# Token-tile turns with a diagonal of roots, and expert slots in the order in which they come free, in a two-block transformer kernel

## The chip, the cores and the metric

The kernel runs on one core of one Trainium2 chip. The metric is the device time of one execution in microseconds, from three runs; one further execution was profiled. The engines are TensorE (PE in the rows), VectorE (DVE), ScalarE (ACT), GpSimd (POOL) and SyncE (SP), which here issues all transfers.

## The reference, cut to what matters

256 tokens of width 1024 pass through two layers of a first block and one hybrid layer of a second, all in float32:

```python
for i in range(2):                      # mixer 0: MLA attention, mixer 1: differential attention
    a = mixer_i(rms_norm(h, norm_g[i, 0]))
    h = h + rms_norm(a, norm_g[i, 1])
    f = conv_ffn(rms_norm(h, norm_g[i, 2]))      # 1024 -> 2 x 2816, conv of 3 tokens, gelu gate, -> 1024
    h = h + rms_norm(f, norm_g[i, 3])
# second block
a = rms_norm(h, g_mix)                  # then a projection by w_in, two attentions, gates, w_out
h = h + mixed @ w_out
h = h + hier_moe(rms_norm(h, g_ffn))    # 32 experts of 1024 -> 512 -> 1024, each token takes 2
out = rms_norm(h, g_final)
```

`rms_norm(x, g)` is `x * rsqrt(mean(x * x) + eps) * g`. The router sends each of the 256 tokens to two experts; the kernel streams all 32 experts' w1, w3 and w2 (2 MB each, 96 matrices).

## The kernel before

**Products.** A weight piece of up to 128x2048 is loaded into `raw` (4 buffers), ScalarE writes its high part and POOL its low part (`high`, `low`, 4 buffers), and TensorE makes each product of three matmuls: high x high, high x low, low x high (`product`, L669 to L671). The activations lie likewise as `xh` and `xl`, transposed, features on the partitions. `low_ready` counts finished pieces, `pieces_used` the pieces that TensorE has read; it is raised by the first product after a piece.

**Stages and turns.** The order of work is written out by hand, once per engine, and `plan()` gives each group of products a bank of PSUM. Between the stages lie turns, named by what they prepare: `x1` (MLA attention to first FFN), `x2` (FFN to differential attention), `x3` (attention to second FFN), `x4` (FFN to the hybrid layer). A turn has these steps. ScalarE squares the four banks of the branch (`out_sums`, L1316), VectorE multiplies each by the gain `gpost` (`post`, L1784), adds the sums and refines the reciprocal root that ScalarE guessed (`refined`, L1709 to L1717), and adds the branch to the residual `h`, one instruction for each tile of 128 tokens (L1796). ScalarE squares `h` (`h_sums`), the root is refined again, and VectorE writes `xn = h * root * gpre` in four halves (`normed`, L1760). TensorE transposes 16 blocks (`x_transposed`, L679), ScalarE copies the high parts (L1347) and VectorE subtracts for the low parts (L1736); then the products of the next stage begin. In `x4` the root isn't in the path: `xn = h * gpre` (`x_gained`), and the root is applied later. Meanwhile TensorE runs 32 dummy products (`keep_clock`, L698). All steps but the first squares are made for both tiles together:

```python
refined(st[:, 16:18], st[:, 18:20])
for t in range(NT):
    dve.scalar_tensor_tensor(h[:, t, :], xn[:, t, :], st[:, 16 + t:17 + t], h[:, t, :],
                             ALU.mult, ALU.add).then_inc(h_ready, 1)
```

The last products of the attention stages finish tile 0's two banks first; the last `down` piece of an FFN goes over the hidden tiles outermost. The gain rows `gpre` and `gpost` are loaded by SyncE (`pre_gains`, `post_gains`), each behind a wait for the last use.

**Expert slots.** The expert matrices go into eight slots of 2 MB, in turn. They overlay the piece buffers: slot 0 is a part of `room`, 1 and 2 are pairs of `raw` buffers, 3 to 6 the four `parts` buffers, 7 is `xspare`. Matrix n goes into slot n modulo 8. `vacated(c)` is SyncE's wait before the first use of a slot; later uses wait for `slots_used`, which TensorE raises when it has read a w1, w3 or w2 pair. SyncE is one queue: a wait holds everything behind it. Experts are taken in pairs (six matrices); TensorE's products are at L1237 and L1262, the gather of tokens at L1187.

## Time and profile before

| what | value |
|---|---|
| median of three runs | 1347.19 us (1344.73 to 1347.28) |
| the profiled execution: time, span | 1345.34 us, 1343.5 us |
| mean granted TensorE clock | 0.994 |
| busy: PE, DVE, ACT, POOL | 95%, 38%, 41%, 43% of the span |
| chain that ended last: PE, transfers, ACT, DVE | 75%, 13%, 4%, 4% |
| POOL's low part of a piece, mean | 4466 ns, 128 of them |
| ScalarE's high part of a piece, mean | 1853 ns, 128 of them |
| HBM read | 339.10 MB |

Shares are averages over very different stages. The chain that ended last says what held the end at each time, and the windows say how busy an engine was in each stage; both are needed here.

### The profile page before, as it was taken

Reading aid. Unit: us, or ns where it says so; the run is one execution under the profiler, and the core shown is the slowest. Engines: PE = TensorE matmul, PEld = TensorE weight load, DVE = VectorE, ACT = ScalarE, POOL = GpSimd, SP = SyncE. Lnnn points to the kernel's source line nnn. Section 1 sums busy time; section 2 is a strip of 40 time slices with the busy share of each in tenths; the row PEclk is TensorE's granted clock in tenths of the full one; section 3 lists DMA queues with packets and bytes.
Section 4 is the critical chain, followed back from the end, with each engine's and each line's share of the span. In section 5 each row is a group of like instructions: output and inputs, shape, how many; then the busy total and the mean of one; then the engine's idle time right before and its main releaser. Section 6 shows DMA issues by size and latency. Waiting matters only on the chain.

```text
span 1343.5 us, 20032 instructions
## 1 busy us (share of the span) xinstructions
PE 1282.8 (95%) x7959; PEld 954.6 (71%) x7959; DVE 509.6 (38%) x1303; ACT 548.0 (41%) x853; POOL 573.2 (43%) x136
## 2 busy tenths in 40 slices
PE   6999999999998899999999999999999999999996
PEld 6867999998987799999878888854444444454442
DVE  2434444445265454444657453421111111121112
ACT  4654555556477465555543664311111111111112
POOL 4722788885944188888567855200000000000001
PEclk9999999999999999999999999999999999999998
DMA  8731666664633266664446444599999999999994
GB/s 270 235 94 63 182 195 188 190 199 144 220 126 95 63 203 196 196 188 165 149 165 203 159 137 161 230 421 426 427 428 428 429 428 429 429 429 428 429 423 189
DMA packets 156933, 341.22 MB, mean 254 GB/s; under 512 B 8537, under 2 KB 119482, under 8 KB 144314
## 3 DMA queue, kind: packets, MB, share of 16 engines
q1 hardware_dynamic: 156858, 340.18, 68.1%
q8 instruction: 53, 0.87, 0.3%
q14 instruction: 22, 0.18, 0.0%
HBM read 339.10 MB, written 1.05 MB: 253 GB/s over the span
## 4 chain that ended last, share of the span: by engine, by line
PE 75%; DMA 13%; ACT 4%; DVE 4%; POOL 2%; issue 1%; SPq 0%; ACTq 0%; DVEq 0%
PE bank L669 16%; PE bank L671 15%; PE bank L670 15%; PE bank L1237 11%; DMA xspare<-in_w 6%; DMA ring<-in_w 6%; PE bank L1262 5%; PE bank L1187 3%; PE bank L768 2%; POOL parts L621 2%; PE bank L679 1%; PE bank L1217 1%; ACT parts L1305 1%; PE bank L1105 1%; PE bank L1121 1%
## 5 line engine op out<-in xcount | busy, mean ns | idle before, releaser
L621 POOL TENSOR_TENSOR parts<-raw,parts 128x2048 fp32r<-128x2048 f32 (+4 forms) x128 | 568.0, 4466 | 290.2 <-ACT parts L1305 290.2
L669 PE MATMUL bank<-xh,parts 128*128 128x256 f32 x1032 | 288.0, 279 | 6.0 <-POOL parts L621 4.0
L670 PE MATMUL bank<-xl,parts 128*128 128x256 f32 x1032 | 285.9, 277 | 0.0
L671 PE MATMUL bank<-xh,parts 128*128 128x256 f32 x1032 | 285.8, 277 | 0.0
L1305 ACT ACTIVATE parts<-raw 128x2048 fp32r<-128x2048 f32 (+4 forms) x128 | 236.1, 1853 | 23.4 <-PE bank L669 8.5
L1237 PE MATMUL bank<-ring,room 128*64 128x512 f32 x768 | 226.1, 594 | 7.1 <-DMA ring<-in_w 4.5
L644 POOL TENSOR_TENSOR xn<-h,gpost 128x512 f32<-128x512 f32 x4 | 4.9, 1270 | 474.7 <-DVE h L2258 474.7
L669 PEld LDWEIGHTS bank<-xh,parts 128*128 128x128 f32 x1032 | 194.2, 188 | 12.6 <-POOL parts L621 4.8
L670 PEld LDWEIGHTS bank<-xl,parts 128*128 128x128 f32 x1032 | 193.8, 188 | 0.8
L671 PEld LDWEIGHTS bank<-xh,parts 128*128 128x128 f32 x1032 | 193.9, 188 | 0.0
L1237 PEld LDWEIGHTS bank<-ring,room 128*64 128x64 f32 x768 | 72.5, 137 | 111.4 <-issue 111.4
L669 PE MATMUL bank<-parts,xh 128*128 128x512 f32 (+5 forms) x304 | 114.7, 377 | 5.8 <-DVE xl L1738 2.2
L1262 PE MATMUL bank<-ring,room 128*64 128x512 f32 x384 | 115.0, 600 | 0.7 <-ACT room L1668 0.7
L671 PE MATMUL bank<-parts,xl 128*128 128x512 f32 (+5 forms) x304 | 112.5, 370 | 0.0
L670 PE MATMUL bank<-parts,xh 128*128 128x512 f32 (+5 forms) x304 | 112.2, 369 | 0.0
L1668 ACT ACTIVATE room<-bank 128x512 f32<-128x512 f32 x16 | 9.6, 597 | 193.5 <-PE bank L1248 193.5
L671 PE MATMUL bank<-parts,hl 128*128 128x512 f32 x192 | 75.6, 394 | 0.0
L669 PE MATMUL bank<-parts,hh 128*128 128x512 f32 x192 | 74.6, 389 | 0.8 <-POOL parts L621 0.8
L670 PE MATMUL bank<-parts,hh 128*128 128x512 f32 x192 | 75.3, 392 | 0.0
L1484 ACT ACTIVATE room<-bank,room 128x256 f32<-128x256 f32 x64 | 32.7, 560 | 102.2 <-PE bank L671 101.0
L1342 ACT ACTIVATE room<-bank 128x512 f32<-128x512 f32 (+1 forms) x75 | 41.1, 581 | 75.9 <-PE bank L679 32.5
L1262 PEld LDWEIGHTS bank<-ring,room 128*64 128x64 f32 x384 | 34.9, 138 | 51.5 <-issue 49.3
(255 smaller groups left out, 1858.9 us busy)
## 6 DMA issues: line engine op xcount, KB each, us to landing
ring<-in_w SPq DMA_DIRECT2D x67, 2048.0 KB, 22.9
raw<-in_ffn_w_up SPq DMA_DIRECT2D x88, 512.0 KB, 4.9
room<-in_w SPq DMA_DIRECT2D x12, 2048.0 KB, 20.3
raw<-in_ffn_w_down SPq DMA_DIRECT2D x44, 512.0 KB, 3.9
xspare<-in_w SPq DMA_DIRECT2D x11, 2048.0 KB, 26.6
raw<-in_w_in SPq DMA_DIRECT2D x40, 512.0 KB, 4.1
raw<-in_diff_w_qkv SPq DMA_DIRECT2D x24, 512.0 KB, 4.6
ring<-in_w SPq DMA_DIRECT2D x10, 1024.0 KB, 24.8
```

Source lines behind the costliest of these rows:

```text
L621: pool.tensor_tensor(low[:, p % PARTS, 0:n], raw[:, p % RING, 0:n], high[:, p % PARTS, 0:n], ALU.subtract).then_inc(low_ready, 1)
L669: first = pe.matmul(out_, a[0], b[0], start=start, stop=False)
L670: pe.matmul(out_, a[0], b[1], start=False, stop=False)
L671: return first, pe.matmul(out_, a[1], b[0], start=False, stop=stop)
L679: ins = pe.transpose(b[0:cols, at:at + rows], src, ident[0:rows, 0:rows])
L768: ins = pe.matmul(b[:, t * S:t * S + S], qs[n][:, t * P:t * P + P], ks[n], start=n == 0, stop=n == len(qs) - 1)
L1187: ins = pe.matmul(bank[2 + k // 4][:, P * (k % 4):P * (k % 4) + P], xn[:, t, P * k:P * k + P], Sel[:, t].rearrange("p e c -> p (e c)"), st ...
L1237: ins = pe.matmul(bank[x][CAP * e:CAP * e + CAP, :], XgT[:, k, CAP * e:CAP * e + CAP], rows_of(j, x, e, k, EF), start=k == 0, stop=k == KT ...
L1262: ins = pe.matmul(bank[1 + hf][CAP * e:CAP * e + CAP, :], hidT[:, k, CAP * e:CAP * e + CAP], rows_of(j, 2, e, k, D)[:, 512 * hf:512 * hf + ...
L1305: act.activation(high[:, p % PARTS, 0:n], raw[:, p % RING, 0:n], ACT.Copy).then_inc(high_ready, 1)
L1342: act.activation(dst, src, func, scale=scale).then_inc(bank_moved[BANK[g]], 1)
L1484: act.activation(fbuf[b][a], bank[b][:, a * S:a * S + S], ACT.Identity, bias=par(3, a), scale=par(1, a)).then_inc(centre, 1)
```

## The change

**Turns.** `post` becomes `turned_over`: gained halves, sums, root and residual of tile 0, then those of tile 1; the last `down` piece of an FFN finishes tile 0 first. In x1 to x3 `xn` and its gain are gone: VectorE writes a diagonal of the tile's roots (`spread_roots`), and TensorE multiplies each 128x128 block of `h` by it (`h_transposed`), which transposes and scales. The gain of the features is now a column (`gcol`, loaded as 32 rows with the parameters and transposed once) and is applied in the high and low parts, which go by chunks of 128x256 (`high_chunks`, `low_chunks`); the next stage waits for one bank at a time. x4 transposes `h` unscaled. The dummy products are 23 in x1 to x3, and 5 and 11 in x4. Four of the six loads of `gpre` are gone, and with them SyncE's waits.

**Slots.** The slots are renumbered in the order in which they come free (third and fourth slot are now `parts` buffers), and the ninth matrix of the first four pairs goes into two free places of 1 MB (`ninth`), once the router has read `xT`, ahead of the wait for its slot. Its slot stays empty for that turn. `cs` now also holds `prow` and `convT`, so that the second place is in one piece.

```diff
-        slots += [pairs_of[tail[2 * x] // 2] for x in range(RING // 2)]
-        slots += [pairs_of[RING // 2 + b] for b in tail]
+        slots += [pairs_of[tail[0] // 2]]
+        slots += [pairs_of[RING // 2 + b] for b in tail[:2]]
+        slots += [pairs_of[tail[2] // 2]]
+        slots += [pairs_of[RING // 2 + b] for b in tail[2:]]
         slots += [xspare[:, :]]
+        NINTH = (1, 1, 0)
+        ninth = [view(4096, HALF), cs[:, C_DIST:C_DIST + HALF]]
...
             def vacated(c):
+                end = W["end"]
                 if c == 0:
                     full(sp, A_["hyb_att"][2][7])
-                elif c < 3:
-                    sp.wait_ge(low_ready, W["end"] - RING + 2 * c)
+                elif c in (1, 4):
+                    sp.wait_ge(low_ready, end - 2 if c == 1 else end)
                 else:
-                    sp.wait_ge(pieces_used, W["end"] - RING + min(c - 3, RING - 1) + 1)
+                    sp.wait_ge(pieces_used, {2: end - 3, 3: end - 2, 5: end - 1}.get(c, end))
...
+                            elif begins and (j, x, e) == NINTH:
+                                full(sp, G["router1"])
+                                for n in range(2):
+                                    sp.dma_start(ninth[n].unsqueeze(1), w[:, 2 * j + e:2 * j + e + 1, HALF * n:HALF * n + HALF]
+                                                 ).then_inc(ninth_here, 16)
+                                continue
+                            elif e == 0 or begins and (j, x) == NINTH[:2]:
                                 sp.wait_ge(slots_used, 12 * four + (3 * j + x - SLOTS // 2 + 1))
...
+            def h_transposed(name, site, scaled, between=0):
+                b = [begin(G[name] + q) for q in range(4)]
+                for t in range(NT):
+                    if t and between:
+                        keep_clock(between, bank[4])
+                    if scaled:
+                        pe.wait_ge(spread_ready, 2 * (site - 1) + t + 1)
+                    else:
+                        pe.wait_ge(h_ready, 2 * (site - 1) + t + 1)
+                    for k in range(KT):
+                        at = S * (k % 2) + P * t
+                        dst, src = b[k // 2][:, at:at + P], h[:, t, P * k:P * k + P]
+                        if scaled:
+                            ins = pe.matmul(dst, src, spread_r[:, t], start=True, stop=True)
+                        else:
+                            ins = pe.transpose(dst, src, ident)
+                        if t == 0 and k == 0:
+                            behind(ins)
+                        if t and k % 2:
+                            end(ins, G[name] + k // 2)
+                late.extend([(2 * q, G[name] + q) for q in range(4)])
...
-            WAIT = 32
+            WAIT = 23
...
-                if k == 4:
-                    while late:
-                        moved(pe, late.pop(0))
+                while late and late[0][0] <= k:
+                    moved(pe, late.pop(0)[1])
...
+                    each = [(x, t, hf) for x in range(2) for t in range(NT) for hf in range(2)]
+                    if stop:
+                        each = [(x, t, hf) for t in range(NT) for x in range(2) for hf in range(2)]
+                    for i, (x, t, hf) in enumerate(each):
+                        if not any(x == y for y, _, _ in each[:i]):
+                            pe.wait_ge(hid_ready, n + (n0 + 1 + x))
+                        first, ins = product(bank[4 + 2 * t + hf][:, :],
+                                             [y[:, (j + x) % 4, t * P:t * P + P] for y in (hh, hl)],
+                                             [y[:, x, 512 * hf:512 * hf + 512] for y in w],
+                                             start and x == 0, stop and x == 1)
+                        behind(first)
+                        if stop and x == 1:
+                            ins.then_inc(ffn_full, 1)
...
-            keep_clock(WAIT, bank[3])
-            x_transposed("x4", 4)
+            keep_clock(WAIT // 4, bank[3])
+            h_transposed("x4", 4, False, WAIT // 2)
...
+                            if nine and (j, x, e) == NINTH and k == KT - 1:
+                                ins.then_inc(arrived[slot_of(*NINTH)[0]], 16)
...
+                    if by_tile:
+                        act.wait_ge(h_squares, 2 * site + t + 1)
+                        guess(st[:, 28 + t:29 + t], st[:, t:t + 1], D)
+                if not by_tile:
+                    act.wait_ge(h_squares, 2 * site + 2)
+                    guess(st[:, dst:dst + 2], st[:, 0:2], D)
...
+            def high_chunks(name, site):
+                for k in range(KT):
+                    g = G[name] + k // 2
+                    full(act, g)
+                    act.activation(xh[:, k, :], bank[BANK[g]][:, S * (k % 2):S * (k % 2) + S], ACT.Copy,
+                                   scale=gain_of(site, k)).then_inc(x_high, 1)
...
+                    squares(st[:, 2 + n:3 + n], bank[b][:, :], view(6400 + 512 * n, 512), post_squares)
+                    if n % 2:
+                        t = n // 2
                         outs_done[0] += 1
-                    squares(st[:, 2 + n:3 + n], bank[b][:, :], view(6400 + 512 * n, 512), post_squares)
-                act.wait_ge(sums_ready, outs_done[0])
-                guess(st[:, 16:18], st[:, 18:20], D)
+                        act.wait_ge(sums_ready, outs_done[0])
+                        guess(st[:, 16 + t:17 + t], st[:, 18 + t:19 + t], D)
...
+            def low_chunks(name, site):
+                for k in range(KT):
+                    g = G[name] + k // 2
+                    x_parts[0] += 1
+                    dve.wait_ge(x_high, x_parts[0] + (1 - k % 2))
+                    ins = dve.scalar_tensor_tensor(xl[:, k, :], bank[BANK[g]][:, S * (k % 2):S * (k % 2) + S],
+                                                   gain_of(site, k), xh[:, k, :], ALU.mult, ALU.subtract)
+                    if k % 2:
+                        ins.then_inc(bank_moved[BANK[g]], 1)
...
+            def half_of(t, src):
+                steps[0] += 1
+                dve.tensor_scalar(st[:, 32 + t:33 + t], src, -0.5 / D, -0.5 * EPS, ALU.mult, ALU.add).then_inc(vec, 1)
+            def root_of(t, y):
+                guesses[0] += 1
+                dve.wait_ge(guessed, guesses[0])
+                dve.wait_ge(vec, steps[0])
+                a = st[:, 48 + t:49 + t]
+                link(dve.tensor_scalar(a, y, y, st[:, 32 + t:33 + t], ALU.mult, ALU.mult))
+                link(dve.tensor_scalar(y, a, 1.5, y, ALU.add, ALU.mult))
+            def turned_over(site, banks, ring_groups):
+                def gained_half(t, hf):
+                    b = banks[2 * t + hf]
+                    dve.wait_ge(post_squares, 4 * site + 2 * t + hf + 1)
+                    x = slice(512 * hf, 512 * hf + 512)
+                    ins = dve.tensor_tensor(xn[:, t, x], bank[b][:, :], gpost[:, x], ALU.mult)
                     ins.then_inc(bank_moved[b] if ring_groups else vec, 1)
-                if not ring_groups:
-                    steps[0] += 4
-                sums = st[:, 2:6].rearrange("p (t h) -> p t h", h=2)
-                dve.tensor_tensor(st[:, 18:20], sums[:, :, 0], sums[:, :, 1], ALU.add).then_inc(sums_ready, 1)
-                dve.wait_ge(sums_ready, site + 1)
-                refined(st[:, 16:18], st[:, 18:20])
-                for g in ring_groups or []:
-                    moved(dve, g)
-                for t in range(NT):
+                    if not ring_groups:
+                        steps[0] += 1
+                def summed(t):
+                    dve.wait_ge(post_squares, 4 * site + 2 * t + 2)
+                    dve.tensor_tensor(st[:, 18 + t:19 + t], st[:, 2 + 2 * t:3 + 2 * t], st[:, 3 + 2 * t:4 + 2 * t],
+                                      ALU.add).then_inc(sums_ready, 1)
+                    dve.wait_ge(sums_ready, 2 * site + t + 1)
+                    half_of(t, st[:, 18 + t:19 + t])
+                def residual(t):
+                    root_of(t, st[:, 16 + t:17 + t])
+                    for g in (ring_groups or [])[2 * t:2 * t + 2]:
+                        moved(dve, g)
                     dve.scalar_tensor_tensor(h[:, t, :], xn[:, t, :], st[:, 16 + t:17 + t], h[:, t, :],
                                              ALU.mult, ALU.add).then_inc(h_ready, 1)
+                dve.wait_ge(gpost_here, 16 * (site + 1))
+                gained_half(0, 0)
+                summed(0)
+                gained_half(0, 1)
+                residual(0)
+                gained_half(1, 0)
+                summed(1)
+                gained_half(1, 1)
+                residual(1)
+            def spread_roots(site):
+                for t in range(NT):
+                    dve.wait_ge(h_squares, 2 * site + t + 1)
+                    half_of(t, st[:, t:t + 1])
+                    root_of(t, st[:, 28 + t:29 + t])
+                    dve.tensor_scalar(spread_r[:, t], ident, st[:, 28 + t:29 + t], None, ALU.mult).then_inc(spread_ready, 1)
+            def x_transposed(name, site):
+                spread_roots(site)
+                low_chunks(name, site)
```

## Rows read from the trace of the kernel before

**Rows 1.** Windows by stage: length, busy us (instructions) by engine, clock, DMA share, GB/s.

```profile
132.50:315.50 183.00, 181.08 (x1320) 170.08 (x1321) 85.19 (x204) 102.92 (x130) 151.26 (x33) 1.00 0.62 189
657.40:865.30 207.90, 205.03 (x1328) 177.03 (x1329) 108.71 (x270) 105.47 (x164) 132.10 (x29) 1.00 0.48 163
890.00:1100.00 210.00, 209.92 (x1148) 99.05 (x1146) 39.12 (x83) 26.90 (x37) 0.00 (x0) 1.00 1.00 427
1100.00:1320.00 220.00, 211.15 (x1134) 101.47 (x1130) 37.04 (x81) 28.18 (x38) 0.00 (x0) 1.00 1.01 426
```

**Rows 2.** TensorE's waits from 130 to 315 us: total, times, longest.

```profile
PE bank L669 <- POOL parts L621: 1.9, 1, 1.9
```

**Rows 3.** Timeline of turn x1: start, us, engine, line, operation [idle before].

```profile
118.44 0.19 ACT L1316 ACTIVATION_READ_ACCUMULATOR room<-bank 128x1 f32 x1
...
120.50 7.46 PE L698 MATMUL bank<-xh 128*128 128x512 f32 x32
...
123.47 2.48 DVE L1796 SCALAR_TENSOR_TENSOR h<-xn,st,h 128x1024 f32<-128x1024 f32 x2
...
126.96 0.18 ACT L1316 ACTIVATION_READ_ACCUMULATOR xn<-h 128x1 f32 x1
...
127.58 0.46 DVE L1714 TENSOR_SCALAR st<-st 128x1 f32<-128x1 f32 x2 [0.19 <-ACT st L1330]
...
128.44 2.74 DVE L1760 SCALAR_TENSOR_TENSOR xn<-h,st,gpre 128x512 f32<-128x512 f32 x4
...
132.47 0.35 PE L669 MATMUL bank<-xh,parts 128*128 128x256 f32 x1 [0.59 <-issue]
```

**Rows 4.** Timeline of turn x4.

```profile
646.36 2.68 DVE L1784 TENSOR_TENSOR xn<-bank,gpost 128x512 f32<-128x512 f32 x4 [3.37 <-ACT room L1316]
...
647.43 7.45 PE L698 MATMUL bank<-xh 128*128 128x512 f32 x32
...
654.71 1.91 PE L679 MATMUL bank<-cs,xn 128*128 128x128 f32 x16
...
657.37 0.36 PE L669 MATMUL bank<-parts,xh 128*128 128x256 f32 x1 [0.75 <-DVE xl L1736]
```

**Rows 5.** Timeline at the end of the first FFN, ahead of turn x2.

```profile
310.67 0.42 DVE L1973 TENSOR_TENSOR hl<-bank,hh 128x256 fp32r<-128x256 f32 x1
...
311.41 0.39 PE L669 MATMUL bank<-parts,hh 128*128 128x512 f32 x1
```

**Rows 6.** ScalarE copies out of PSUM, by form: ns min/median/max.

```profile
L1342 ACT ACTIVATE room<-bank x75: 378/597/624, 36.1 to 870.2; 128x512 f32<-128x512 f32 x70, 128x256 f32<-128x256 f32 x5
L1342 ACT ACTIVATE room<-bank,st x4: 677/686/688, 709.8 to 757.0; 128x512 f32<-128x512 f32 x4
```

**Rows 7.** TensorE's timeline at the first gather of the experts.

```profile
877.67 3.81 PE L1187 MATMUL bank<-room,xn 128*128 128x128 f32 x32 [1.52 <-DVE room L2223]
```

**Rows 8.** Timeline of the first tile after turn x1.

```profile
138.40 1.02 ACT L1484 ACTIVATE room<-bank,convT 128x256 f32<-128x256 f32 x2 [5.88 <-PE bank L671]
...
139.46 0.87 DVE L1957 SCALAR_TENSOR_TENSOR room<-bank,convT,room 128x255 f32<-128x255 f32 x2 [5.89 <-ACT room L1484]
```

**Rows 9.** SyncE's issues of expert matrices, from narrow timelines.

```profile
888.59 0.33 SPq L578 DMA_DIRECT2D room<-in_w  x1
...
896.57 0.80 SPq L578 DMA_DIRECT2D ring<-in_w  x2
...
908.22 0.80 SPq L578 DMA_DIRECT2D ring<-in_w  x2
```

**Rows 10.** Narrow windows, columns as in rows 1.

```profile
890.00:891.00 1.00, 1.00 (x8) 0.37 (x6) 0.37 (x2) 0.00 (x0) 0.00 (x0) 1.00 0.61 197
910.00:911.00 1.00, 1.00 (x6) 0.29 (x4) 0.00 (x0) 0.00 (x0) 0.00 (x0) 1.00 0.94 344
446.00:449.00 3.00, 3.00 (x8) 2.35 (x8) 0.15 (x1) 0.69 (x2) 2.65 (x1) 0.50 0.00 0
```

**Rows 11.** TensorE's timeline ahead of the slow stretch at 446.

```profile
445.44 0.50 PE L669 MATMUL bank<-parts,xh 128*128 128x512 f32 x1 [1.56 <-DVE xl L1738]
```

131 lines of the change are left out of this document (56 added, 75 removed).

## The prediction

> **What bounds the kernel now.** I read the granted clock first (0.994 over the span), then the chain of work that ended last, then busy time by windows. The windows show two regimes [rows 1]. From the first FFN to the router TensorE is busy 181.1 of 183.0 us and 205.0 of 207.9 us, and the waits that remain are small and hang on its own earlier progress: the one of the first FFN, 1.9 us, is for the third piece's low part [rows 2], which ScalarE begins only after the first tile's products, so it moves with them. In the expert stage the transfers run at 427 GB/s from 890 us to the end while TensorE is busy 209.9 of 210.0 us and later 211.2 of 220 us: from about 1100 us each pair waits a little for data, so the end is set by the expert stream. One matrix is 2.097 MB, so 4.9 us at that rate. The stream is held by TensorE at its start: a slot is refilled when products free it.
>
> Between stages lie four turns, in which TensorE runs only 32 dummy products, transposes and nothing else. In turn x1 the dummies start at 120.50 and the first product of the next stage at 132.47: 11.97 us [rows 3]. x2 and x3 have the same 11.97 in their timelines. x4 takes 657.37 - 647.43 = 9.94 us, as its gain and transposes don't wait for a root [rows 4]. The reader should see that everything between is a single chain over DVE and ScalarE: residual, squares, root, gain, transpose, high part, low part, each for both tiles before the next begins.
>
> **The turn, part by part.** Times are from the first dummy.
> 1. *The roots of the branch by tile.* The second square of tile 0 is read at 118.63, -1.87 [rows 3]. DVE then has, in order: add and half 0.35, gained half 0.67 (four in 2.68 [rows 4]), root 0.55, residual 1.24 (two in 2.48 [rows 3]), and for tile 1 gained half 0.67, add and half 0.35, gained half 0.67, root 0.55, residual 1.28. The sum is 6.33, so both residuals end at +4.46 instead of +5.45 (123.47 + 2.48). The root for both tiles took 128.44 - 127.58 = 0.86 [rows 3]; with one tile two dependent operations remain, bounds 0.43 and 0.86, and 0.55 is nearer the lower, because it is two latencies without the second issue. Squares of tile 0 lie beside all this. Queued behind ScalarE's new waits is only this chain.
>    For x2 and x4 the last down piece is reordered, tile 0 first. That gives them tile 0's banks as early as x1 and x3 have them. It asks for the second hidden tile two products earlier: low part done at 311.09, third product at 311.41 [rows 5], so 0.3 us to spare, the same in both FFNs.
> 2. *The diagonal of roots.* After the residual ScalarE squares tile 1: it ended 1.19 us after the residual (126.96 + 0.18 against 125.95) [rows 3]. Then guess to DVE 0.44 (127.14 to 127.58), root 0.55, and a 128x128 diagonal, for which I take 0.3, between half of a pair of one-column operations (0.23 [rows 3]) and one of 255 columns (0.475 [rows 8]). Diagonal ready: 4.46 + 1.19 + 0.44 + 0.55 + 0.3 = +6.94. The four 512-wide gains (2.74 in all) leave the path.
> 3. *Scaled transposes.* These are full products of 128 columns; 32 such in the gather took 3.81 [rows 7], 0.119 each, the same as transposes [rows 4]. Tile 0's eight lie in the wait. After tile 1's first two (0.24 + 0.15 to the end) a bank is full: +7.35.
> 4. *Chunks of 128x256 with a gain column.* ScalarE's plain copy of that size is 0.378 and a scale from a column adds 0.09 at 512 (0.686 against 0.597) [rows 6], so 0.47, a pitch of 0.37 (two with scale and bias 0.46 apart, 0.56 long [rows 8]). DVE's like operation is 0.475 long at a pitch of 0.40 [rows 8]. A bank has two chunks and DVE waits for both highs: 0.37 + 0.47 + 0.40 + 0.475 + hand-overs 0.15 = 1.87. TensorE starts at +9.22 instead of +11.97, 2.75 sooner.
> 5. *Then it takes the banks as they come.* Six products last 0.70, a bank's two lows 0.80: three times 0.10 is lost. Net 2.45 per turn. Slow end: chunks as L1484 (0.56, pitch 0.46) and pairs at 0.95, diagonal 0.5: 1.6. Fast end: chunk times without the column's surcharge, no loss: 2.9. I take 2.4; three turns 7.2 (4.8 to 8.7).
> 6. *x4.* Tile 1 is transposed at the later of +4.46 and +4.63 (16 dummies of 0.23 and 8 transposes of 0.119), first bank +5.05, plus 1.87: +6.92 against 9.94, minus 0.1: 2.9 (2.3 to 3.2). Squares and scales follow the chunks on ScalarE and come perhaps 1.5 us sooner, not 3; the third piece of w_in still has some 1.5 us of cover, and if the cover is gone up to 1 us of the 2.9 is lost.
>
> *What is removed and moved on queues.* Four 512 KB gain loads go, four loads of 8 rows come, a gain copy and 32 more transposed rows ride with the parameters in the attention stage. SyncE no longer waits for the normed halves behind the gain loads, so the weights of the next stage are issued up to 6 us sooner; TensorE isn't waiting for them, so this counts nothing, 0 to 0.3 us either way.
>
> **The slots.** The new order lets the third and fourth slot fill while wout's products run, where the transfers stood idle; the ninth matrix is loaded beside the eight. Both are full before the first pair's w1 is used up, so nothing of this shortens the stream unless later releases keep pace. Before, matrices 9 and 10 were issued at 888.59, 11 and 12 at 896.57, 13 and 14 at 908.22 [rows 9]. The stream ran dry near 890 (197 GB/s in that us) and nearly again at 910 (344) [rows 10]. So an issue becomes data 1.9 us later, and the 13th came exactly when 9 to 12 were done: 890.5 + 4 x 4.9 = 910.1 against 908.22 + 1.9 = 910.1. With the ninth already there, 10 runs 890.5 to 895.4, 11 and 12 from 898.4 to 908.2, and then the stream waits for the same issue at 908.22, because slots 5 and 6 hold w2 of the first pair, and TensorE frees them at its own pace. The saved 4.9 us turn into idle transfers. I take 0.2 us (0 to 4.9, the latter if releases didn't bind).
>
> **The clock.** The granted clock stayed at 1.00 in all four turns, although after the dummies TensorE does only transposes. It did fall once: after 1.56 us of idle behind one short group of transposes [rows 11] three us ran at 0.50, that is 1.2 GHz [rows 10]. Three us at half speed lose 1.5, and with the edges 1.6. The new turns have 9 fewer dummies, which end at +5.25; then 0.95 of products, a gap of 0.5, 0.95, a gap near 1.3. That is less bare time than before (dummies ended +7.5, products at +11.97).
> The Trainium skill, "TensorE: Matmul & The Clock Gate", Part 4, says that transposes don't count as busy for the gate, and Part 1 that idle stretches throttle it. By that rule the scaled transposes, being plain products, would hold the clock better than the old ones, while x4 with fewer dummies would be exposed: the sum would be 1.6 us less for x4. This trace agrees with the second in one place and shows no fall after the old turns.
>
> **Sum.** 7.2 + 2.9 + 0.2 = 10.3 us. The profiled execution took 1345.34 us (span 1343.5 and 1.8 around it): 1335.0. The median of the three runs, 1347.19, is 1.85 above it, so in medians 1336.9. I predict 1336.0, between them.
>
> **Rivals.**
> - *The clock falls in the turns.* For: less dummy work, the fall at 446. Against: shorter bare stretches. Three falls cost 4.8: 1341. Chance 0.13.
> - *The stages behind take part of it back* (ScalarE's chunks are eight for four, so its splits lag TensorE's start). For: the lag in x2 and x4. Against: the waits of the stages are few [rows 2]. Half is lost: 1341. Chance 0.17.
> - *The ninth matrix counts in full.* It needs the 13th's release not to bind; the 908.22 speaks against it. 1331.3. Chance 0.10.
> - *Slower: the stream's rate.* From the 9th matrix on 88 take 88 x 4.9 = 431 us. The slots now fill in another order and the first transfers overlap other work; if they collide for good and the rate falls by 2.4% (427 to 417 GB/s), the 10.3 us are gone, and beyond that the kernel is slower; at 4% it loses 17 and takes 1353. Against: the same areas hold the slots, and both long windows show 427 and 426 [rows 1]. Chance 0.03.
> - *The change doesn't shorten the turns* (a root or bank wait as long as the gain took): 1346. Chance 0.05.
> - My forecast, 0.52, has its own range 1333 to 1339.
>
> The 80% range is 1331.5 to 1341.5. A difference within 0.2% (2.7 us) can't be told from none here. Faster 0.93, same 0.04, slower 0.03.
>
> **What would show it.** Right: from first dummy to first product 9.2 us in x1 to x3 and 6.9 in x4; TensorE's busy share between turns unchanged; the router about 10 us sooner; transfers idle for about 4 us before the 10th matrix and 2 us before the 13th; the rate at 427 again. Wrong: a clock below 1.00 behind a turn, a wait on POOL's parts longer than 1.9 us, a stage whose length grew, or an expert stage shorter by 4 us from the router to the end.

## The result, and the profile after

The changed kernel takes 1357.59 us (median of 5 runs, 1354.38 to 1360.01) against 1345.58 us for the kernel before on the same chip (1344.20 to 1347.28): a ratio of 1.0081, 95% interval 1.0065 to 1.0097. It was predicted faster, 1336.0 us; it is slower by 12 us, or 0.8%. The profiled execution took 1355.69 us, its span 1353.8 us.

The windows go from mark to mark of TensorE: first dummy product, first product of the next stage, and so on. Below are, of the kernel after, the first FFN, turn x2, the second FFN, the hybrid stage up to the router, and the stretch from the end of the router's products to the first expert product. Columns as in [rows 1].

```profile
130.49:320.43 189.94, 187.99 (x1320) 175.80 (x1321) 87.59 (x208) 103.51 (x132) 151.67 (x33) 0.99 0.59 180
320.43:332.18 11.75, 9.23 (x56) 7.78 (x55) 8.55 (x24) 6.39 (x18) 0.06 (x1) 1.00 0.35 116
...
465.32:655.24 189.92, 187.99 (x1320) 175.80 (x1321) 87.51 (x211) 104.30 (x134) 150.50 (x33) 0.99 0.57 176
...
662.67:880.06 217.39, 214.44 (x1376) 184.12 (x1376) 115.34 (x289) 111.32 (x175) 132.00 (x29) 1.00 0.53 186
880.06:891.26 11.20, 9.55 (x56) 8.55 (x55) 5.70 (x32) 5.07 (x11) 0.00 (x0) 0.85 1.00 422
```

The first FFN issues the same 1320 products as before, TensorE is as busy (188.0 of 189.9 us, before 181.1 of 183.0 [rows 1]), it waits for nothing new, and yet it takes 6.9 us longer. No waiting engine is to be found: the products themselves follow each other more slowly. The timeline of a quiet stretch shows it. First the kernel before, then the kernel after, each with 18 products from the first row's start to the second row's:

```profile
200.02 0.28 PE L669 MATMUL bank<-xh,parts 128*128 128x256 f32 x1
...
202.06 0.28 PE L669 MATMUL bank<-xh,parts 128*128 128x256 f32 x1
```

```profile
200.04 0.28 PE L690 MATMUL bank<-xh,parts 128*128 128x256 f32 x1
...
202.16 0.28 PE L690 MATMUL bank<-xh,parts 128*128 128x256 f32 x1
```

That is 2.04 / 18 = 113 ns from product to product before and 2.12 / 18 = 118 ns after. In the groups of the profile's page the durations follow (the mean ns of one stands just ahead of the last bar). First the kernel before, then the kernel after:

```profile
L669 PE MATMUL bank<-xh,parts 128*128 128x256 f32 x1032 | 288.0, 279 | 6.0 <-POOL parts L621 4.0
...
L669 PE MATMUL bank<-parts,hh 128*128 128x512 f32 x192 | 74.6, 389 | 0.8 <-POOL parts L621 0.8
```

```profile
L690 PE MATMUL bank<-xh,parts 128*128 128x256 f32 x1032 | 292.1, 283 | 5.8 <-POOL parts L642 3.8
...
L690 PE MATMUL bank<-parts,hh 128*128 128x512 f32 x192 | 76.1, 396 | 0.4 <-POOL parts L642 0.4
```

The pitch, the time from one product's start to the next one's, is over all products of the first FFN at full clock 114.0 ns for the 256 wide and 228.9 for the 512 wide before, 117.7 and 233.4 after. There are some 1056 and 264 of them: 1056 x 3.7 + 264 x 4.5 = 5.1 us. The other 1.7 us of the 6.9 are a clock fall, below. The table puts the whole span together, in us; its last two columns are experiments told further down.

| stretch | before | after | gcol last | and one-tensor add |
|---|---|---|---|---|
| start to first dummy | 120.5 | 120.9 | 120.9 | 120.2 |
| turn x1 | 12.0 | 9.6 | 9.6 | 9.8 |
| first FFN | 183.1 | 189.9 | 183.2 | 183.1 |
| turn x2 | 12.0 | 11.8 | 13.7 | 10.6 |
| differential attention | 125.1 | 123.6 | 123.2 | 122.0 |
| turn x3 | 12.0 | 9.6 | 9.7 | 9.8 |
| second FFN | 182.8 | 189.9 | 185.1 | 185.1 |
| turn x4 | 10.0 | 7.4 | 7.9 | 7.0 |
| hybrid stage to the router's end | 214.4 | 217.4 | 214.4 | 214.4 |
| to the first expert product | 9.7 | 11.2 | 11.3 | 9.7 |
| experts to the end | 462.1 | 462.5 | 460.6 | 462.0 |
| span | 1343.5 | 1353.8 | 1339.6 | 1333.6 |

So the turns did give 7.5 us, and the other stretches took 17.8 back. Turn x1 in the timeline of the kernel after (compare [rows 3]):

```profile
120.93 5.39 PE L744 MATMUL bank<-xh 128*128 128x512 f32 x23
...
123.66 1.28 DVE L1885 SCALAR_TENSOR_TENSOR h<-xn,st,h 128x1024 f32<-128x1024 f32 x1
...
126.16 3.76 PE L731 MATMUL bank<-score,h 128*128 128x128 f32 x32
...
127.05 0.29 DVE L1904 TENSOR_SCALAR score<-cs,st 128x128 f32<-128x128 f32 x1
128.62 3.03 ACT L1425 ACTIVATE xh<-bank,gcol 128x256 fp32r<-128x256 f32 x8 [2.16 <-PE bank L731]
...
130.51 0.36 PE L690 MATMUL bank<-xh,parts 128*128 128x256 f32 x1 [0.59 <-DVE xl L1827]
```

The residual of the second tile ends at 124.94, 4.0 us behind the first dummy (predicted 4.46), its diagonal is there at +6.4 (6.94), the first bank is full at +7.7 (7.35), and the first product comes 1.89 us behind that (1.87). The 32 rows of the scaled transposes are 16 products (`h_transposed` issues eight for each tile): each is recorded as two of 0.12 us. That is why tile 0's eight, begun at 126.16, hold the engine until 128.0, though tile 1's diagonal is there at 127.34, and tile 1's first two end 0.5 behind 128.0.

Turn x2 is another matter. GpSimd, then three operations of VectorE:

```profile
315.87 4.61 POOL L642 TENSOR_TENSOR parts<-raw,parts 128x2048 fp32r<-128x2048 f32 x1
...
318.57 1.93 DVE L1876 TENSOR_TENSOR st<-st 128x1 f32<-128x1 f32 x1
...
323.76 0.15 DVE L1876 TENSOR_TENSOR st<-st 128x1 f32<-128x1 f32 x1
...
328.74 0.29 DVE L1904 TENSOR_SCALAR score<-cs,st 128x128 f32<-128x128 f32 x1
```

VectorE's add of two one-column sums (L1876) takes 1.93 us. The same operation for tile 1 takes 0.15. It ends when GpSimd's subtraction ends: 315.87 + 4.61 = 320.48. Both its inputs lie in SBUF, as do both inputs of GpSimd. Behind it is the whole chain of tile 0, and the second diagonal is ready at 329.0, 8.6 us behind the first dummy at 320.4 and not 6.4 as in turn x1. The Trainium skill, "SBUF — State Buffer", section "Who interferes with whom", has the rule: an instruction of VectorE with two SBUF inputs and one of GpSimd that reads SBUF exclude each other, and the later waits for the whole of the other. This trace agrees, with 1.93 us here and 0.66 us in turn x4.

The clock, in four us each behind turn x1, at the first gather of the experts and behind turn x3 (the column ahead of the last two is the granted clock):

```profile
145.00:149.00 4.00, 4.00 (x24) 4.00 (x23) 3.02 (x9) 1.92 (x3) 4.00 (x2) 0.57 0.94 260
885.00:889.00 4.00, 2.98 (x14) 3.01 (x15) 2.05 (x12) 1.28 (x1) 0.00 (x0) 0.60 1.01 428
479.00:483.00 4.00, 4.00 (x21) 4.00 (x22) 3.02 (x9) 2.76 (x4) 4.00 (x1) 0.58 0.76 211
```

Each of these is a stretch of 3.4 us at 0.50, the 1.2 GHz level, and costs 1.7 us. The first follows TensorE's longest wait in that stage:

```profile
144.15 0.38 PE L690 MATMUL bank<-xh,parts 128*128 128x256 f32 x1 [1.92 <-POOL parts L642]
```

The kernel before had the same wait [rows 2] and no fall there; it had two falls at 425 and 446 us [rows 10], which this kernel has not. The gather took 5.34 us for its 32 products, before 3.81 [rows 7]:

```profile
886.02 5.34 PE L1235 MATMUL bank<-room,xn 128*128 128x128 f32 x32 [1.52 <-DVE room L2336]
```

### The profile page after: what moved, and what is told of

It is laid out like the page before. It is cut to its first block, busy times and chain, and to the rows that moved or that the text cites. A ratio compares the mean times of both kernels' runs of the same rounds, so it can differ in the third digit from the quotient of the medians.

```text
span 1353.8 us, 20067 instructions
## 1 busy us (share of the span) xinstructions
PE 1294.0 (96%) x7964; PEld 965.3 (71%) x7964; DVE 507.5 (37%) x1314; ACT 552.1 (41%) x876; POOL 573.0 (42%) x136
## 3 DMA queue, kind: packets, MB, share of 16 engines
HBM read 337.02 MB, written 1.05 MB: 250 GB/s over the span
## 4 chain that ended last, share of the span: by engine, by line
PE 77%; DMA 11%; ACT 5%; DVE 4%; POOL 2%; issue 1%; SPq 0%; ACTq 0%; DVEq 0%
PE bank L690 16%; PE bank L692 15%; PE bank L691 15%; PE bank L1292 12%; DMA ring<-in_w 6%; PE bank L1320 6%; DMA xspare<-in_w 4%; PE bank L1235 3%; PE bank L813 2%; POOL parts L642 2%; PE bank L1265 1%; ACT parts L1364 1%; PE bank L744 1%; PE bank L700 1%; PE bank L1153 1%
## 5 line engine op out<-in xcount | busy, mean ns | idle before, releaser
L690 PE MATMUL bank<-xh,parts 128*128 128x256 f32 x1032 | 292.1, 283 | 5.8 <-POOL parts L642 3.8
L692 PE MATMUL bank<-xh,parts 128*128 128x256 f32 x1032 | 290.0, 281 | 0.0
L691 PE MATMUL bank<-xl,parts 128*128 128x256 f32 x1032 | 289.5, 281 | 0.0
L1557 ACT ACTIVATE room<-bank,room 128x256 f32<-128x256 f32 x64 | 32.7, 561 | 113.9 <-PE bank L692 113.9
```

The source lines that it names most:

```text
L690: first = pe.matmul(out_, a[0], b[0], start=start, stop=False)
L691: pe.matmul(out_, a[0], b[1], start=False, stop=False)
L692: return first, pe.matmul(out_, a[1], b[0], start=False, stop=stop)
L1557: act.activation(fbuf[b][a], bank[b][:, a * S:a * S + S], ACT.Identity, bias=par(3, a), scale=par(1, a)).then_inc(centre, 1)
```

## The experiments

There are thirteen more kernels. "Distance" in what follows is the byte address in a partition of x's halves (`xh`, `xl`; but for one kernel `hh`, `hl` have the same) less that of the weight pieces' halves (`parts`), modulo 256. In the 256 wide products the weight piece is loaded and x streamed; in the 512 wide ones `hh` or `hl` (or x) is loaded and the weight piece streamed. The tiles are laid out in the order of their allocation. In the kernel before `parts` begins at 49280 and `xh` at 152640: the distance is 192. In the changed kernel `gcol`, 32 columns or 128 bytes, is allocated between them, `xh` begins at 152768, and the distance is 64. `cs`, `prow` and `convT` swap places with `subT` but fill the same space.

### The layout alone, and the change without it

before_pad128:

```
+        pad = sb("pad", [P, 32])
         wr = sb("wr", [P, KT, NG + NE])
```

> The kernel before with one unused SBUF tile of 128 bytes per partition ahead of the router's weights, so that h, xn, the halves of x and of the hidden rows, st and the rest lie 128 bytes higher, exactly where they lie in the changed kernel; no instruction is added or taken away. Theory A (addresses: where the operands lie sets the pitch of the products): 256 wide products go from 113 to 114 ns at 117 to 118 in the FFN stages, 512 wide from 229 to 233, FFN stages 5 us longer each, hybrid stage 3, sum 12 to 15 us: 1357 to 1361. Theory B (the new turns restart TensorE in a slower rhythm): nothing, 1345.6 +- 1. Theory C (the two moved transfers and the new order of slots): nothing as well.

Measured: 1362.84 us, ratio 1.0119 [1.0093, 1.0146] against the kernel before. One unused tile makes it slower by 17 us. Its first FFN, with no clock fall in it:

```profile
132.38:320.61 188.23, 186.29 (x1320) 173.96 (x1321) 85.22 (x204) 102.89 (x130) 151.56 (x33) 1.00 0.60 185
```

Pitches 117.8 and 233.3, those of the changed kernel; it comes out 5 us above that kernel because it has the longer turns of before. It lies 2 us above the expected range: in its hybrid stage the clock is down for 6.8 us, which costs 3.4. Without that stretch both FFN stages are 5 us longer than before, the hybrid stage 2.8 and the differential stage 0.2.

after_gcol_last:

```
-        gcol = sb("gcol", [P, 4 * KT])
         ...
         ss_o, rs_o = sb("ss_o", [P, 16]), sb("rs_o", [P, 16])
+        gcol = sb("gcol", [P, 4 * KT])
```

> The changed kernel with its tile of gains, gcol, allocated behind all others, so that every operand of a product lies where it lies in the kernel before; every instruction is kept. Theory A: pitches back at 113 to 114 and 229, both FFN stages some 5 us shorter than in the changed kernel (184 to 185, the clock fall behind each turn stays), hybrid 3 shorter: 1342 to 1345, with x1, x3 and x4 at 9.6, 9.6 and 7.4 us and x2 at 11.8. Theory B or C: 1357.6 as the changed kernel.

Measured: 1340.92 us, ratio 0.9966 [0.9947, 0.9984]. The same instructions as in the changed kernel, and 1.0081 has become 0.9966: some 15 us, and 1 us less than the range expected. Pitches 113.9 and 228.9:

```profile
130.54:313.77 183.23, 181.31 (x1320) 170.25 (x1321) 87.58 (x208) 103.58 (x132) 151.36 (x33) 1.00 0.60 186
```

Theory A holds, in that the place of the tiles makes the 15 us, and B falls: neither the new turns nor the restart after them make them. Turn x2 was expected at 11.8 and took 13.7, since the whole chain comes as late as in the changed kernel and the clock falls in it as well:

```profile
309.67 4.63 POOL L642 TENSOR_TENSOR parts<-raw,parts 128x2048 fp32r<-128x2048 f32 x1
...
311.94 2.37 DVE L1876 TENSOR_TENSOR st<-st 128x1 f32<-128x1 f32 x1
...
321.62 5.28 PE L731 MATMUL bank<-score,h 128*128 128x128 f32 x32 [2.45 <-DVE score L1904]
```

turns_only (slots, their waits and the ninth matrix as before; `gcol` last):

```
-        slots += [pairs_of[tail[0] // 2]]
-        slots += [pairs_of[RING // 2 + b] for b in tail[:2]]
-        slots += [pairs_of[tail[2] // 2]]
-        slots += [pairs_of[RING // 2 + b] for b in tail[2:]]
+        slots += [pairs_of[tail[2 * x] // 2] for x in range(RING // 2)]
+        slots += [pairs_of[RING // 2 + b] for b in tail]
...
-                    pair(base + j, j, fours, first=first and j == 0, opens=j == 0, start=j == 1,
-                         nine=first and j == NINTH[0])
+                    pair(base + j, j, fours, first=first and j == 0, opens=j == 0, start=j == 1)
```

> The turns of the changed kernel alone: the expert slots are as before (eight blocks, their order and waits), gcol lies last. Theory A, with the slots worth 0.2 us at most: within 1 us of the kernel with gcol last and all parts, 1342 to 1345. Theory C (slots or the ninth matrix slow the stages): faster than that one by 5 or more.

Measured: 1341.32 us, ratio 0.9966 [0.9951, 0.9980]: the same as with all parts.

slots_only (the reverse of that diff on the kernel before, with `cs`, `prow` and `convT` as one tile):

> The slots and the ninth matrix of the changed kernel alone, with the turns of before; cs, prow and convT are one tile, no operand of a product moves. Theory A and B: 1345.6 +- 1, first product of the experts to the end 462 us. Theory C: 1350 or more.

Measured: 1345.46 us, ratio 1.0001 [0.9982, 1.0020]. From the first expert product to the end it takes 461.9 us, before 462.1. Theory C falls, and the slots are worth nothing, as predicted. The windows of one microsecond of the kernel with `gcol` last show where the ninth matrix's head start goes (the first row is the clock fall of its turn x2, the others the transfers in the last column):

```profile
321.00:325.00 4.00, 3.38 (x17) 3.41 (x18) 1.37 (x6) 0.94 (x3) 0.00 (x0) 0.57 0.76 226
885.00:886.00 1.00, 1.00 (x9) 0.31 (x5) 0.00 (x0) 0.00 (x0) 0.00 (x0) 1.00 0.00 0
893.00:894.00 1.00, 1.00 (x6) 0.32 (x3) 0.20 (x1) 0.00 (x0) 0.00 (x0) 1.00 0.08 33
907.00:908.00 1.00, 1.00 (x8) 0.38 (x6) 0.00 (x0) 0.00 (x0) 0.00 (x0) 1.00 0.36 98
```

The stream stands still at 885 and nearly so at 893 and 907 us, 6 to 28 us behind the first expert product at 879.05: SyncE waits there for `slots_used`, for slots that TensorE has not freed.

### What about the layout counts

before_pad64 and before_pad256 are the first diff with `[P, 16]` and `[P, 64]`, before_pad192 with `[P, 48]`. pad128_behind_x has `[P, 32]` ahead of `hh` and `hl`. Two more move the weight pieces as well, by a tile ahead of `raw` and `parts`, which is there from then on:

```
+        front = sb("front", [P, 32])
         with nc.sbuf_tensor("raw", [P, RING, PIECE], F32) as raw, \
...
+        pad = sb("pad", [P, 16])     # all_at_0;  parts_at_0: [P, 32]
         wr = sb("wr", [P, KT, NG + NE])
```

> As the kernel before with 128 bytes of padding, but 64: h, xn, the halves of x and of the hidden rows and all behind them lie 64 bytes higher. Theory A1 (only certain offsets are good, and the kernel before happened to have one): slow as with 128 bytes, pitches 118 and 233, 1358 to 1364. Theory A2 (distance of the operands to each other counts in units of 128 bytes or more): as the kernel before, 113 to 114 and 229, 1345.6.

> The same with 256 bytes. If the pattern repeats every 256 bytes: as the kernel before, 1345.6, pitches 113 to 114 and 229. If it does not: 118 and 233, 1358 to 1364. Against theory A in every form: any result within 1 us of the kernel before together with the same for 64.

> The padding of 128 bytes stands behind the halves of x (xh, xl) and ahead of those of the hidden rows (hh, hl), so that x, h and xn stay where they are and only hh, hl, st, room and what follows move. If it is the operand of the product itself whose place counts: the 256 wide products of the FFN (x against up) stay at 113 to 114 ns, the 512 wide ones (hidden rows against down) go from 229 to 233, FFN stages +1.2 us each: 1348 to 1350. If it is the place of what VectorE and ScalarE write beside them (room, the scratch of the depthwise convolution): both widths go to 118 and 233: 1356 or more.

> The kernel before with 192 bytes of padding ahead of the router's weights. Byte address of xh per partition modulo 256: 64 in the kernel before, 128 with 64 bytes (pitches 119.9 and 227.7), 192 with 128 bytes (117.8 and 233.3), 64 again with 256 bytes (113.6 and 228.9), 0 here; the weight pieces stay at 128. Theory A3 (the place modulo 256 of the operands sets the pitch): a fourth pair of pitches that differs from all three; if a product is best where its streamed operand begins on a multiple of 256, the 256 wide pitch falls under 113 and the time under 1345. If only the distance to the pieces counts (here 128), it may go either way, 1335 to 1366.

> 128 bytes of padding ahead of the weight pieces and 64 ahead of the router's weights: pieces and halves of x and of the hidden rows all begin on a multiple of 256 bytes. If the place itself counts (an operand that begins on 256 reads without a penalty): both widths are at their lowest, towards the 109 ns that 256 wide products show in the attention stages (some 110 and 218): 1315 to 1335. If the distance between the two operands counts: as before_pad64 with 0 in place of its 0 (there the pieces lie at 128 and x at 128): 120 and 228, 1362 to 1366.

> 128 bytes of padding ahead of the weight pieces and 128 more ahead of the router's weights: the pieces go from 128 to 0 modulo 256, x and the hidden rows stay at 64. If only the place of x and the hidden rows counts: as the kernel before, 113.6 and 228.9, 1345 to 1348. If the distance of the two counts (64 - 0 = 64 here, as 192 - 128 with 128 bytes of padding): 118 and 233, 1358 to 1364.

The last two kernels shift the fastest version (below) by 32 and 224 bytes:

> The kernel with gcol last and the one-tensor add, with 32 bytes of padding ahead of the router's weights. Distance from the weight pieces to x modulo 256: so far 192 gave 113.6 and 228.9 ns, 0 gave 119.9 and 227.7, 64 gave 117.8 and 233.3, 128 gave 119.8 and 231.5, whatever the two places themselves; here it is 224. If the reads collide in blocks of 64 bytes: something between those of 192 and 0, 116 to 117 and 228: 1345 to 1350. If only the block in which the operand begins counts: as 192, 1337.6. If 224 is better than 192: under 1335.

> The same with 224 bytes: the distance is 160 modulo 256, between 128 (119.8 and 231.5) and 192 (113.6 and 228.9). Between the two: 116 to 118 and 230: 1345 to 1352. If the best distance is not a multiple of 64, this or the one with 32 bytes is under 1335.

Measured (bytes modulo 256; mean pitches in ns over the first FFN at full clock; ratio to the executions of the kernel before that ran beside each, 95% interval):

| kernel | parts at | x at | distance | 256 wide | 512 wide | us | ratio |
|---|---|---|---|---|---|---|---|
| before | 128 | 64 | 192 | 114.0 | 228.9 | 1345.6 | 1 |
| before_pad256 | 128 | 64 | 192 | 113.6 | 228.9 | 1347.8 | 1.0003 [0.9982, 1.0024] |
| after_gcol_last | 128 | 64 | 192 | 113.9 | 228.9 | 1340.9 | 0.9966 [0.9947, 0.9984] |
| after | 128 | 192 | 64 | 117.7 | 233.4 | 1357.6 | 1.0081 [1.0065, 1.0097] |
| before_pad128 | 128 | 192 | 64 | 117.8 | 233.3 | 1362.8 | 1.0119 [1.0093, 1.0146] |
| parts_at_0 | 0 | 64 | 64 | 117.4 | 233.3 | 1359.7 | 1.0098 [1.0063, 1.0134] |
| before_pad64 | 128 | 128 | 0 | 119.9 | 227.7 | 1365.8 | 1.0127 [1.0102, 1.0152] |
| all_at_0 | 0 | 0 | 0 | 119.9 | 227.7 | 1363.4 | 1.0110 [1.0072, 1.0148] |
| before_pad192 | 128 | 0 | 128 | 119.8 | 232.6 | 1364.4 | 1.0127 [1.0100, 1.0153] |
| shift224 | 128 | 32 | 160 | 117.8 | 233.0 | 1354.4 | 1.0084 [1.0056, 1.0112] |
| shift32 | 128 | 96 | 224 | 118.3 | 233.2 | 1355.6 | 1.0076 [1.0050, 1.0102] |
| pad128_behind_x | 128 | 64; hh 192 | 192; hh 64 | 115.9 | 233.1 | 1353.8 | 1.0048 [1.0029, 1.0067] |

For before_pad192 the two expectations written after it have 231.5; that leaves out the 30 of its 263 products that stand 240 or 241 ns apart, and with them it is 232.6.

The first FFN in one window each, of before_pad64, all_at_0, parts_at_0 and before_pad256:

```profile
132.28:322.69 190.41, 188.55 (x1320) 177.89 (x1321) 85.22 (x204) 102.84 (x130) 151.41 (x33) 0.99 0.60 182
```

```profile
132.48:322.86 190.38, 188.52 (x1320) 177.87 (x1321) 85.16 (x204) 102.82 (x130) 151.24 (x33) 0.99 0.58 182
```

```profile
133.17:321.19 188.02, 185.90 (x1320) 173.48 (x1321) 85.25 (x204) 102.90 (x131) 151.66 (x33) 1.00 0.59 185
```

```profile
132.08:316.54 184.46, 182.28 (x1320) 171.32 (x1321) 85.24 (x204) 102.95 (x130) 151.39 (x33) 0.99 0.61 186
```

The pairs decide. Kernels with the same distance and different places agree: before_pad64 and all_at_0 (distance 0) within 0.03 us over 190 us, parts_at_0 and before_pad128 (64) within 0.2 over 188; one with 256 bytes more is as before (its 1.4 us are a clock fall, its mean clock is 0.99). Moving the pieces alone, x staying where it was, is as slow as moving x alone (with the pieces move `ring`, `cs` and the gains, with x move `h`, `xn`, `st` and `room`; the distance is that of the two groups). So over an FFN stage the pitch hangs on the distance modulo 256 and not on where either operand lies. The timeline at distance 0, 18 products: 2.16 / 18 = 120 ns.

```profile
199.98 0.28 PE L671 MATMUL bank<-xl,parts 128*128 128x256 f32 x1
...
202.14 0.28 PE L671 MATMUL bank<-xl,parts 128*128 128x256 f32 x1
```

The finer steps show that 192 is the best of the six distances tried, and that 32 bytes away from it the 256 wide products are back at 118. Both expectations for these steps were missed upwards (1355.6 for 1345 to 1350, 1354.4 for 1345 to 1352): they are no better than at 64, so neither of the two places tried between multiples of 64 gains anything. before_pad64 fitted neither of its theories: slow as A1 had it, but with pitches of its own. The hope that all at multiples of 256 would be best, 1315 to 1335 us, was wrong by 28 us and more. The 109 ns of the attention stages, on which it leant, are not there for such products: those of 128x256 against `parts` stand 113 to 120 ns apart there too.

pad128_behind_x is a half miss. The 512 wide products, whose operand `hh` or `hl` moved, went to 233.1 as expected and the time to 1353.8, above the expected 1348 to 1350. The 256 wide ones did not move and yet average 115.9: some stretches of them are at 113 and some at 118. The stage:

```profile
132.28:318.45 186.17, 184.25 (x1321) 172.14 (x1322) 85.29 (x204) 102.91 (x131) 151.67 (x33) 1.00 0.61 187
```

This is a finer pattern than the means show, and it runs through the FFN stages of all kernels at 192 and 64. The 256 wide products come in runs of some 96, and each run settles, but for its first dozen or two products, at 113.3 ns or at 117.8 and keeps to it; the next run, behind a wait of TensorE or a group of 512 wide products, may have the other pace. Behind the first such group of an FFN stage the distance decides: the nine long runs of each stage are all at 113 in the six kernels at 192, and all at 118 in the three at 64. pad128_behind_x, with x at 192 and `hh` at 64, takes the two in turn, four runs fast and five slow. So the products' own two operands don't decide it alone; that the group ahead of them, whose operand moved, counts as well is the likely reading and not tested by itself. Ahead of the first 512 wide group either pace occurs at either distance: the kernel before starts its first FFN with 118, and parts_at_0, at distance 64, with 113. In the differential stage the two even change sides. Here are 18 products each of the kernel before (192) and of before_pad128 (64):

```profile
340.07 0.28 PE L670 MATMUL bank<-xl,parts 128*128 128x256 f32 x1
...
342.19 0.28 PE L670 MATMUL bank<-xl,parts 128*128 128x256 f32 x1
```

```profile
340.06 0.28 PE L672 MATMUL bank<-xh,parts 128*128 128x256 f32 x1
...
342.10 0.28 PE L672 MATMUL bank<-xh,parts 128*128 128x256 f32 x1
```

It is 118 ns at distance 192 and 113 at 64. The 512 wide products are simpler, and pad128_behind_x tells their cause within one kernel: in the FFN stages, where they load `hh` and `hl` (64), they stand 233.1 ns apart, and in the differential and the hybrid stage, where they load x (192), 229.5 and 229.0. `room` and `st` moved in all of these stages, so it isn't their place that counts.

### The add of turn x2

add_one_tensor (on after_gcol_last):

```
-                    dve.tensor_tensor(st[:, 18 + t:19 + t], st[:, 2 + 2 * t:3 + 2 * t], st[:, 3 + 2 * t:4 + 2 * t],
+                    dve.tensor_scalar(st[:, 18 + t:19 + t], st[:, 2 + 2 * t:3 + 2 * t], st[:, 3 + 2 * t:4 + 2 * t], None,
                                       ALU.add).then_inc(sums_ready, 1)
```

> The changed kernel with gcol last, and the sum of a tile's two half sums of squares written as an operation with one tensor and one scalar column in place of one with two tensors. Theory D (VectorE's operation with two SBUF tensors waits until GpSimd's subtraction ends, 2.37 us in turn x2): the add takes 0.15, the residual of tile 0, which has two SBUF tensors as well, begins no earlier than the end of GpSimd's subtraction; turn x2 goes from 13.7 to 10.5 to 11.5 us, since the clock does not fall in it either; x4 0.3 shorter: 1336.5 to 1338.5, against 1340.9 with gcol last alone. Rival (the wait is that of the engine's semaphores or of ScalarE): x2 stays at 13.7, 1340.9.

Measured: 1337.64 us, ratio 0.9927 [0.9906, 0.9948]: the fastest version, faster than both kernels. GpSimd and VectorE in turn x2:

```profile
309.00 4.62 POOL L642 TENSOR_TENSOR parts<-raw,parts 128x2048 fp32r<-128x2048 f32 x1
...
311.28 0.21 DVE L1876 TENSOR_SCALAR st<-st 128x1 f32<-128x1 f32 x1
...
312.95 1.76 DVE L1885 SCALAR_TENSOR_TENSOR h<-xn,st,h 128x1024 f32<-128x1024 f32 x1
...
316.88 1.28 DVE L1885 SCALAR_TENSOR_TENSOR h<-xn,st,h 128x1024 f32<-128x1024 f32 x1
```

The add takes 0.21 us under the same subtraction of GpSimd. The residual of tile 0 (L1885), which has two SBUF tensors, now takes 1.76 where the one of tile 1 takes 1.28; its row begins while GpSimd still runs (309.00 + 4.62 = 313.62) and not, as expected, behind it, and is 0.48 longer instead. Turn x2 took 10.6 us, x4 7.0 (0.8 shorter, where 0.3 was expected) and the clock fell in neither; the gather escaped its fall as well, so part of the 0.4% is that. TensorE's scaled transposes came early enough to run at full clock:

```profile
319.33 3.81 PE L731 MATMUL bank<-score,h 128*128 128x128 f32 x32 [0.82 <-DVE score L1904]
323.73 0.36 PE L690 MATMUL bank<-xh,parts 128*128 128x256 f32 x1 [0.59 <-DVE xl L1827]
```

## Why the prediction was wrong

**The step that failed** is the one that costed the stages between the turns at nothing, "TensorE's busy share between turns unchanged". The busy share was unchanged, and it told nothing: a busy engine can be slow. The working went through every instruction of the change, and its sum, 7.2 + 2.9 + 0.2, has no term for where the tiles lie, though `gcol` stands ahead of the activations in the kernel. It did name "a stage whose length grew" as a sign of being wrong, and that is the sign that came. Moving x by 128 bytes against the weight pieces costs, by the table's columns after and gcol last: 5.0 us in the first FFN (189.9 - 183.2, less 1.7 for the fall that only the first holds), 4.8 in the second (a fall in both), 3.0 in the hybrid stage, and 2.1 in the differential stage (123.6 against 123.2, of which 1.7 is a fall). That is 14.9 us of span, and the two medians differ by 16.7. before_pad128 shows it from the other side with some 13 us (5.2, 5.0, 2.8, and only 0.2 in the differential stage). So the FFN and hybrid stages are the solid part, some 13 us in both pairs; in the differential stage 0.7 of the 2.1 are 512 wide products, and the rest is the pace of the 256 wide ones, which there is found at either distance.

**The forecast for the change itself** is to be read from after_gcol_last, 1340.9 and not 1336.0. That lies within the predicted range of 1331.5 to 1341.5, but not by its sum: the turns gave half of what they were to give. The terms:
- *Turns x1 and x3:* predicted 2.4 shorter each, measured 2.3 to 2.4, but that is in part luck. By the sum the first product was to come 9.2 us behind the first dummy, 2.75 sooner, and 0.3 was to be lost behind it; it came at 9.6, and 0.2 is lost (the first FFN of after_gcol_last). Within the turn the residuals came 0.45 sooner than in the sum and the diagonal 0.5 sooner, but the first full bank came 1.3 us behind the diagonal and not 0.4, since each scaled transpose takes two records of 0.12 us. The row of 32 products in the gather [rows 7] had been read as 32 of 128 columns; the gather issues 16, each recorded twice.
- *Turn x2:* predicted 2.4 shorter. Measured 0.2 shorter in the changed kernel and 1.8 longer in after_gcol_last: the add that waits for GpSimd, and then the clock. This is the largest miss within the turns, 2 to 4 us. In the kernel before the add stood for both tiles 1.5 us behind the first dummy; the new order brings it 1.9 us ahead of it, and there GpSimd's subtraction still runs, until the dummies begin. The sum had placed every operation of VectorE earlier without asking what GpSimd does at the new place. With the wait taken out the turn is 1.4 shorter than before, still 1.0 less than predicted.
- *Turn x4:* predicted 2.9 (with the net of the banks). Measured 2.5 in the changed kernel, whose add is 0.66 us long there, 2.1 in after_gcol_last, whose add is 1.05 us long, and 2.9 with the one-tensor add.
- *Slots and ninth matrix:* predicted 0.2; alone they measure 0.3, with an interval from 2.4 faster to 2.7 slower, and beside the turns 0.4 (1340.9 against 1341.3), which is less than can be told. The reason given, that later releases bind, is what the idle windows at 885, 893 and 907 us show.
- *The clock:* given 0.13 as a rival for the turns. A fall did come in turn x2 of after_gcol_last, where the chain was late, and none in the other turns; turn x4, for which the prediction set out a loss of 1.6 us, had none in any kernel. But falls moved from kernel to kernel elsewhere: ahead of the experts before has two (425, 446; the prediction had seen only the second), the changed kernel three (145, 480, 886), after_gcol_last four (321, 424, 475, 874) and add_one_tensor one (470), at 1.7 us each. In the profiled executions that is 3.4 us against after_gcol_last and 1.7 in favour of add_one_tensor.
- *Slower by the stream's rate*, the rival on the other side, had no part: from the first expert product to the end 462.5 us against 462.1.

Added up for after_gcol_last in the traces: turns -5.0 (predicted -10.1), differential stage -1.9 (a fall fewer), first FFN +0.2, second FFN +2.3 and gather +1.6 (a fall more in each), start +0.4, experts -1.6: -3.9 us of span.

**What stays open.** Why the distance counts, and why 192 is good, the runs don't show. That the weight load of one product and the streamed rows of another read SBUF at once and get in each other's way would fit, since the pitch depends on both addresses together, but this was argued and not measured by itself. Distances 32 and 96 were not tried. What picks the pace of the 256 wide products ahead of the first 512 wide group, and how such a group sets the pace of those behind it, was not found, nor why some waits of 1.9 us bring a clock fall and others not.

## What to carry to other kernels

A new tile is a change to every kernel instruction whose operand lies behind it: allocate additions last, or pin the distance between the tiles of the weights and those of the activations, and when a stage slows with the same counts and waits, compare starts of the same products first. Try a few paddings of 32 to 224 bytes in a kernel bound by TensorE: here they span 20 us of 1345. And where VectorE's small operations stand on a critical chain beside GpSimd, give them one SBUF tensor and a scalar column rather than two tensors.

## What the runs showed of the hardware

- The mean pitch of 128x128 products with fp32r operands at full clock over an FFN stage follows the distance of their two operands modulo 256 bytes. 256 wide: 113.6 to 114.0 ns at 192, 117.4 to 117.8 at 64, 117.8 at 160, 118.3 at 224, 119.8 to 119.9 at 0 and 128. 512 wide: 228.9 at 192, 233.3 to 233.4 at 64, 233.0 at 160, 233.2 at 224, 227.7 at 0 and 232.6 at 128. The best for one width isn't the best for the other.
- At 192 and at 64 the 256 wide products know the same two paces, 113.3 and 117.8 ns, each for nearly all of a run of some 96. Behind the 512 wide products of an FFN stage the distance decides which (108 runs in six kernels and 54 in three); ahead of them, and in the differential stage, both were seen at both.
- The Trainium skill, "SBUF — State Buffer", section "Who interferes with whom", lists TensorE's two read ports, for the streamed operand and for the weight load, as independent and says that TensorE never waits on anyone. Waits on other engines were not put to the test here, but the two operands of the products are not independent of each other: 6 ns of 114, by the table above.
- A wait of VectorE for GpSimd shows as a long instruction and not as idle time: a one-column add of 1.93 us and 2.37 us, and 0.21 us with one tensor operand.
- A product of 128x128 by 128 columns with plain fp32 operands, as in the scaled transposes, is recorded as two of 0.118 us each (16 issued, 32 rows, 3.76 us).
